# The second dense layer of a two-block transformer kernel: gates and ups in one phase and downs in another, each by seven products instead of eight

## The reference

```python
def swiglu(h, wg, wu, wd):
    return (jax.nn.silu(h @ wg) * (h @ wu)) @ wd
...
        h = rms_norm(x, norm_ffn_g[i]) * (1 + sc2) + sh2
        x = x + g2 * swiglu(h, ffn_w_gate[i], ffn_w_up[i], ffn_w_down[i])
    return rms_norm(x, final_norm_g)
```

## Time and profile before

| | us |
|---|---|
| median of 3 runs | 1472.97 (1471.86 to 1478.15) |
| the profiled execution | 1474.04 |
| its span | 1472.3 |
| TensorE matmul busy | 1382.5 (94%) |
| VectorE busy | 811.6 (55%) |
| ScalarE busy | 248.1 (17%) |
| mean granted clock of TensorE | 0.981 |

### The profile page before, as it was taken

One profiled execution on the slowest core, in us unless ns is written; L12 is line 12 of the kernel. 1 busy time (PEld: TensorE's weight loads), 2 busy tenths in 40 slices (PEclk: granted clock), 3 DMA queues, 4 the chain that ended last, 5 costly groups with the idle time before them and its releaser, 6 DMA issues. The chain is left out here.

```text
span 1472.3 us, 18919 instructions
## 1 busy us (share of the span) xinstructions
PE 1382.5 (94%) x7561; PEld 1018.4 (69%) x7561; DVE 811.6 (55%) x1405; ACT 248.1 (17%) x530; POOL 259.0 (18%) x342
## 2 busy tenths in 40 slices
PE   5999999988757999999999999999999999999997
PEld 1877655644333888778888888777776868777774
DVE  2458785332223677853544674888744963544432
ACT  2221211000001211322435101000002032000001
POOL 5078010000001100543436304000021000000000
PEclk9999999998888999999999999999999999999999
DMA  9976788899999588846773456988853633545530
GB/s 345 324 253 230 273 341 328 366 415 416 417 418 369 184 299 290 298 142 157 182 174 117 143 171 201 333 323 326 311 183 103 215 94 115 168 151 168 166 120 29
DMA packets 176055, 355.57 MB, mean 242 GB/s; under 512 B 7289, under 2 KB 137040, under 8 KB 158560
## 3 DMA queue, kind: packets, MB, share of 16 engines
q1 hardware_dynamic: 166720, 313.64, 59.8%
q0 software_dynamic: 9248, 40.71, 9.5%
HBM read 352.58 MB, written 1.74 MB: 241 GB/s over the span
## 5 line engine op out<-in xcount | busy, mean ns | idle before, releaser
L1823 PE MATMUL PS<-HT,ring 128*128 128x256 f32 x1152 | 258.3, 382 | 0.1
L1823 PEld LDWEIGHTS PS<-HT,ring 128*128 128x128 f32 x1152 | 215.5, 190 | 36.0 <-issue 7.9
L2724 PE MATMUL PS<-ring,hid 128*128 128x512 f32 x320 | 143.5, 592 | 0.0
L2724 PEld LDWEIGHTS PS<-ring,hid 128*128 128x128 f32 x320 | 60.8, 190 | 60.3 <-issue 58.4
L2718 PE MATMUL PS<-HT,ring 128*128 128x256 f32 x464 | 101.6, 379 | 0.0
L2718 PEld LDWEIGHTS PS<-HT,ring 128*128 128x128 f32 x464 | 87.8, 190 | 11.8
L1264 PE MATMUL PS<-ring_extra,slot_rows 128*32 128x256 f32 x576 | 54.6, 431 | 27.7 <-DMA ring_extra<-in_expert_w_gate 7.9
L1541 DVE TENSOR_TENSOR X<-X,PS 128x1024 f32<-128x1024 f32 x14 | 17.1, 1221 | 111.6 <-PE PS L1317 111.6
L2747 PE MATMUL PS<-ring,half_sums 128*128 128x256 f32 x288 | 68.1, 379 | 0.0
L2747 PE MATMUL PS<-ada_stage,half_sums 128*128 128x256 f32 x288 | 68.1, 379 | 0.0
L2747 PE MATMUL PS<-ring,HT 128*128 128x256 f32 x288 | 65.2, 379 | 0.0
(11 more groups left out here) (653 smaller groups left out, 2283.4 us busy)
## 6 DMA issues: line engine op xcount, KB each, us to landing
ring<-in_hy_w_in SPq DMA_DIRECT2D x40, 1024.0 KB, 7.5
ring_extra<-in_w_ada SPq DMA_DIRECT2D x24, 1024.0 KB, 8.5
ada_stage<-in_ada_w POOLq DMA_DIRECT2D x24, 1024.0 KB, 7.6
ring<-in_ffn_w_gate SPq DMA_DIRECT2D x22, 1024.0 KB, 5.7
ring<-in_ffn_w_up SPq DMA_DIRECT2D x22, 1024.0 KB, 5.9
ring<-in_ffn_w_down SPq DMA_DIRECT2D x22, 1024.0 KB, 5.1
ring_extra<-in_expert_w_down SPq DMA_DIRECT2D x18, 1024.0 KB, 22.9
ring_extra<-in_expert_w_up SPq DMA_DIRECT2D x18, 1024.0 KB, 20.1
```

Source lines behind the costliest of these rows:

```text
L1823: mm = pe.matmul(dst, w[:, k, half * P:(half + 1) * P], HT[:, k, :], start=(k == 0), stop=(k == KT - 1))
L2724: mm = pe.matmul(PS[:, 4 + 2 * i + h, :], hid[:, par, f, i * P:(i + 1) * P], w[:, f, h * 512:(h + 1) * 512], start=first and f == 0, stop= ...
```

## The change

In the second dense layer all 11 chunks take seven products for gate and up, and their products lie in banks 0 to 3 for even chunks and 4 to 7 for odd ones (`split_bank`). The downs are no longer mixed in. The turned rows of all chunks are kept (`hid_T`, in the memory of the finished accumulator `acc`), and so are four sums of halves of them (`hid_half`, 5, 4 and 2 chunks at a time). Then come all downs, with tokens, the 256 hidden and the 1024 columns in two halves each: seven products of one matmul of 128 x 512 per chunk, accumulated over the chunks in seven banks, in six groups of one or two chunks (`DOWN_GROUPS`). VectorE makes four sums of halves of each down weight, 512 wide, one of them in place. At the end `split_last` combines the seven banks into the four pieces of x. Chunk 10's rows are turned inside the first group of downs. The weights arrive in the order g0, u0, g1, u1, up to u10, then d0 to d10, and SP's loop is unrolled. The sums of chunk 0's weights are placed before the gating of the second pointwise product. A semaphore of an earlier stage becomes one that is given back after its stage.

```diff
-segment("ffn1", [ffn_source(1)(k, e) for k, e in expert_order(FFN_CHUNKS)])
+SPLIT_ORDER = [(k, e) for e in range(FFN_CHUNKS) for k in "gu"] + [("d", e) for e in range(FFN_CHUNKS)]
+segment("ffn1", [ffn_source(1)(k, e) for k, e in SPLIT_ORDER])
...
-sem("d_c"), pool_dma_sem("d_fetched"), sem("d_summed"), sem("d_cols"),
+sem("d_c"), sem("d_fetched"), sem("d_summed"), sem("d_cols"),
...
+down_ready = sem("d_ready")
+hid_T = carve(acc[:].rearrange("p a b -> p (a b)"), 0, [FFN_CHUNKS, 2, S])
+hid_half = carve(stage_conv, 0, [4, FFN_CHUNKS, P])
+down_sum = [(tap_blocks[:].rearrange("p a b c -> p (a b c)")[:, 0:12 * CW], wsum[:, 0].rearrange("p j k n -> p (j k n)"),
+             wsum[:, 1].rearrange("p j k n -> p (j k n)"))[b].rearrange("p (e j n) -> p e j n", e=2, j=3)
+            for b in range(3)]
+last_rows = tap_blocks[:].rearrange("p a b c -> p (a b c)").rearrange("p (a n) -> p a n", a=8)
...
 def chunk(f, kind, e):
-    return FFN_BASE[f] + order.index((kind, e))
+    return FFN_BASE[f] + (order, SPLIT_ORDER)[f].index((kind, e))
+
+ROWS_0 = 1 + 7 * NSEV
+HALF_SUMS = ROWS_0 + 2
+DOWN_GROUPS = ((0, 1), (2, 3), (4, 5), (6, 7), (8,), (9, 10))
+HALF_GROUPS = ((0, 5), (5, 9), (9, 11))
+DOWN_ORDER = ("P2", "P1", "P6", "P5", "P3", "P7", "P4")
+DOWN_BANK = {"P2": 4, "P1": 5, "P6": 6, "P5": 7, "P3": 0, "P7": 1, "P4": 2}
+
+def split_summed(e):
+    return ROWS_0 + 1 if e == 0 else split_row(e - 1, 1)
+
+def split_row(e, nth):
+    return HALF_SUMS + 1 + 7 * e + nth + 1
+
+def split_bank(e, name):
+    at = ("P1", "P2", "P5", "P3", "P6", "P4", "P7", "TURN").index(name)
+    return PS[:, 4 * (e % 2) + at // 2, at % 2 * CW:(at % 2 + 1) * CW]
...
-ffn(1, ffn_source(1))
+send_until(sp, FFN_BASE[1] + len(SPLIT_ORDER))
...
+def split_turn(e, m):
+    if m == 0:
+        pe.wait_ge(hid_ready, FFN_CHUNKS + e + 1)
+        pe.wait_ge(combined, split_row(e, 4))
+    else:
+        pe.wait_ge(silu_ready, ACT_MARKS[1, e + 1, ("move", 0)])
+    for i in range(TT):
+        mm = pe.transpose(split_bank(e, "TURN")[:, i * P:(i + 1) * P], hid_rows[:, e % 2, i, m * P:(m + 1) * P],
+                          ident[:])
+    mm.then_inc(sevens, 1)
+
+def split_gate_up(e, norm):
+    n_g, n_u = chunk(1, "g", e), chunk(1, "u", e)
+    gate, up = w_slot(n_g), w_slot(n_u)
+    half = lambda ap, h: [ap[:, 4 * h + k, :] for k in range(4)]
+    rows = lambda h, i: [HT[:, 4 * h + k, i * P:(i + 1) * P] for k in range(4)]
+    hs7 = lambda j: [hsum[:, j, k, :] for k in range(4)]
+    ws7 = lambda j: [wsum[:, (e + 1) % 2, j, k, :] for k in range(4)]
+    to = lambda name: split_bank(e, name)
+    arrive(pe, n_g)
+    arrive(pe, n_u)
+    pe.wait_ge(combined, split_summed(e))
+    if e == 0:
+        for name, h, done in (("P1", 0, left), ("P2", 1, right)):
+            for k in range(KT // 2):
+                pe.wait_ge(done, 4 * norm + k + 1)
+                mm = pe.matmul(to(name), rows(h, 0)[k], half(gate, h)[k], start=(k == 0), stop=(k == KT // 2 - 1))
+        mm.then_inc(used, 1)
+        pe.wait_ge(combined, HALF_SUMS)
+    else:
+        if e >= 2:
+            pe.wait_ge(combined, split_row(e - 2, 6))
+        product(to("P2"), rows(1, 0), half(gate, 1))
+        product(to("P1"), rows(0, 0), half(gate, 0)).then_inc(used, 1)
+    product(to("P5"), hs7(0), ws7(0))
+    if e:
+        split_turn(e - 1, 0)
+    else:
+        pe.wait_ge(combined, HALF_SUMS + 1)
+    product(to("P3"), hs7(3), half(up, 1))
+    if e:
+        split_turn(e - 1, 1)
+    product(to("P6"), hs7(1), ws7(1)).then_inc(sevens, 1)
+    if e >= 2:
+        pe.wait_ge(silu_ready, ACT_MARKS[1, e - 1, ("move", 1)])
+    product(to("P7"), hs7(2), half(up, 0)).then_inc(used, 1)
+    pe.wait_ge(combined, split_row(e, 2))
+    product(to("P4"), rows(1, 1), ws7(2)).then_inc(sevens, 1)
+
+def split_down(gi):
+    group = DOWN_GROUPS[gi]
+    for e in group:
+        arrive(pe, chunk(1, "d", e))
+    pe.wait_ge(down_ready, DOWN_MARKS["weights", gi])
+    pe.wait_ge(down_ready, DOWN_MARKS["rows", [e1 > group[-1] for _, e1 in HALF_GROUPS].index(True)])
+    if gi == 0:
+        pe.wait_ge(combined, split_row(LAST_E - 1, 6))
+        pe.wait_ge(silu_ready, ACT_MARKS[1, LAST_E, ("move", 1)])
+    for name in DOWN_ORDER:
+        if gi == 0 and name == "P3":
+            split_turn(LAST_E, 0)
+            pe.wait_ge(combined, split_row(LAST_E, 6))
+        if gi == 0 and name == "P7":
+            split_turn(LAST_E, 1)
+        for at, e in enumerate(group):
+            w, sums = w_slot(chunk(1, "d", e), D), down_sum[gi % 3][:, at]
+            a = lambda i, m: hid_T[:, e, m, i * P:(i + 1) * P]
+            b = lambda m, h: w[:, m, h * 512:(h + 1) * 512]
+            lhs, rhs = {"P1": (a(0, 0), b(0, 0)), "P2": (a(0, 1), b(1, 0)), "P3": (hid_half[:, 3, e], b(1, 1)),
+                        "P4": (a(1, 1), sums[:, 2]), "P5": (hid_half[:, 0, e], sums[:, 0]),
+                        "P6": (hid_half[:, 1, e], sums[:, 1]), "P7": (hid_half[:, 2, e], b(0, 1))}[name]
+            mm = pe.matmul(PS[:, DOWN_BANK[name], :], lhs, rhs, start=(e == 0), stop=(e == LAST_E))
+            if name == "P4":
+                mm.then_inc(used, 1)
+            elif e == LAST_E:
+                mm.then_inc(downed, 1)
...
-ffn(1, 2)
+for e in range(FFN_CHUNKS):
+    split_gate_up(e, 2)
+for gi in range(len(DOWN_GROUPS)):
+    split_down(gi)
...
-ffn(1)
+for e in range(FFN_CHUNKS + 1):
+    if e <= LAST_E:
+        act.wait_ge(combined, split_row(e, 0))
+        act.activation(gate_act[:, e % 2, 0], gate_pre[:, 0], ACT.Silu).then_inc(silu_ready, 1)
+    if e:
+        for m in range(2):
+            act.wait_ge(sevens, PE_MARKS[1, e, ("turn", m)])
+            act.activation(hid_T[:, e - 1, m, :], split_bank(e - 1, "TURN"), ACT.Copy).then_inc(silu_ready, 1)
+    if e <= LAST_E:
+        act.wait_ge(combined, split_row(e, 6))
+        act.activation(gate_act[:, e % 2, 1], gate_pre[:, 1], ACT.Silu).then_inc(silu_ready, 1)
+act.wait_ge(downed, 3 + 2)
+act.activation(last_rows[:, 0, :], PS[:, DOWN_BANK["P1"], :], ACT.Copy).then_inc(silu_ready, 1)
...
+def split_sum_weights(e):
+    for n in (chunk(1, "g", e), chunk(1, "u", e)):
+        dve.wait_ge(landed[slots[n]], 16 * turns[n])
+    if e >= 2:
+        dve.wait_ge(sevens, PE_MARKS[1, e - 2, "P4"])
+    gate, up = w_slot(chunk(1, "g", e)), w_slot(chunk(1, "u", e))
+    t1, t2, t4 = (wsum[:, (e + 1) % 2, j] for j in range(3))
+    step(dve.tensor_tensor(t1, up[:, 0:4, :], gate[:, 0:4, :], ALU.subtract))
+    step(dve.tensor_tensor(t2, up[:, 4:8, :], t1, ALU.subtract))
+    step(dve.tensor_tensor(up[:, 0:4, :], up[:, 4:8, :], up[:, 0:4, :], ALU.subtract))
+    dve.tensor_tensor(t4, gate[:, 4:8, :], t2, ALU.subtract).then_inc(combined, 1)
+
+def split_sum_down(gi):
+    for at, e in enumerate(DOWN_GROUPS[gi]):
+        n = chunk(1, "d", e)
+        dve.wait_ge(landed[slots[n]], 16 * turns[n])
+        if gi >= 3:
+            dve.wait_ge(used, chunk(1, "d", DOWN_GROUPS[gi - 3][-1]) + 1)
+        w = w_slot(n, D)
+        t1, t2, t4 = (down_sum[gi % 3][:, at, j] for j in range(3))
+        b11, b12, b21, b22 = (w[:, m, h * 512:(h + 1) * 512] for m in range(2) for h in range(2))
+        step(dve.tensor_tensor(t1, b12, b11, ALU.subtract))
+        step(dve.tensor_tensor(t2, b22, t1, ALU.subtract))
+        step(dve.tensor_tensor(b12, b22, b12, ALU.subtract))
+        last = dve.tensor_tensor(t4, b21, t2, ALU.subtract)
+        if e == DOWN_GROUPS[gi][-1]:
+            last.then_inc(down_ready, 1)
+
+def split_halve_rows(at):
+    e0, e1 = HALF_GROUPS[at]
+    dve.wait_ge(silu_ready, ACT_MARKS[1, e1, ("move", 1)])
+    a11, a12, a21, a22 = (hid_T[:, e0:e1, m, i * P:(i + 1) * P] for i in range(TT) for m in range(2))
+    out = lambda j: hid_half[:, j, e0:e1, :]
+    step(dve.tensor_tensor(out(0), a21, a22, ALU.add))
+    step(dve.tensor_tensor(out(2), a11, a21, ALU.subtract))
+    step(dve.tensor_tensor(out(1), out(0), a11, ALU.subtract))
+    dve.tensor_tensor(out(3), a12, out(1), ALU.subtract).then_inc(down_ready, 1)
+
+def split_combine(e):
+    of = lambda name: split_bank(e, name)
+    dve.wait_ge(used, chunk(1, "g", e) + 1)
+    step(dve.tensor_copy(gate_pre[:, 0], of("P2")))
+    dve.tensor_tensor(gate_pre[:, 0], of("P1"), gate_pre[:, 0], ALU.add).then_inc(combined, 1)
+    if e < LAST_E:
+        split_sum_weights(e + 1)
+    else:
+        dve.wait_ge(combined, split_row(e, 0))
+        dve.sem_inc(combined, 1)
+        split_sum_down(0)
+    dve.wait_ge(sevens, PE_MARKS[1, e, "P6"])
+    step(dve.tensor_copy(up_pre[:, 0], of("P1")))
+    dve.tensor_tensor(up_pre[:, 0], of("P6"), up_pre[:, 0], ALU.add).then_inc(combined, 1)
+    dve.wait_ge(combined, split_row(e, 2))
+    step(dve.tensor_tensor(up_pre[:, 1], of("P5"), up_pre[:, 0], ALU.add))
+    dve.tensor_tensor(up_pre[:, 1], of("P3"), up_pre[:, 1], ALU.add).then_inc(combined, 1)
+    dve.wait_ge(combined, split_row(e, 3))
+    dve.wait_ge(silu_ready, ACT_MARKS[1, e, ("gate", 0)])
```

(83 more changed lines are left out.)

## The result

The changed kernel takes 1468.34 us (median of 8, 1466.74 to 1469.60), the kernel before 1475.74 in the runs beside it (8, 1471.86 to 1478.15): a ratio of 0.9946, 95% interval 0.9933 to 0.9960. The forecast was 1466.0 from a median of 1472.97, a ratio of 0.9953.

A forecast was written before the change was run, and what follows sets the result against it. TensorE was taken to bound the stage, VectorE having over half its time free. Products -12.01, waits +2.66 and end +2.33 gave -7.02 us, so 1466.0 us (-0.47%), range 1462.8 to 1470.6.

The forecast's parts named there:

- The products: TensorE's work in the second dense layer: fewer gate, up and down matmuls, two more chunks' rows turned; together -12.01 us.
- Steady chunks: First-phase chunks other than 0, 8 and 10: period 12.53 us, no wait, 0.25 us to spare before P4.
- Three waits: TensorE waits before P4 for VectorE's up row sum in chunks 0, 8 and 10: +1.16, +0.96, +0.54, sum +2.66 us.
- the 0.32: Delay from the end of VectorE's row sum to P4's start: 0.10 handoff plus 0.22 us weight load.
- The variant in that step: If TensorE resumes without the 0.22 us load, waits before P4 in chunks 0, 8 and 10 sum to 2.0 us.
- rival 1: Small waits before P4 are less, 2.66 falling to about 0.5 us; time 1463.8 us; chance 0.12.
- The downs: Second phase, six groups of down products: VectorE never the later one, loads with some 9 us of cover, no wait.
- rival 4: Loads of the downs land late, chunk 10's sums 7.8 us late; time 1473.8 us; chance 0.02.
- The end: Last add to x starts 3.25 us after T, TensorE's last issue, by nine VectorE steps from P3; before 0.92; +2.33.
- Rival 2: The 0.25 us margin before P4 is missing, so every steady chunk waits; +3.5 us, time 1469.5; chance 0.20.
- Rival 3: Short waits lower TensorE's clock to 0.91 in the first phase or the downs too; 1479.6 or 1486.2 us; chance 0.03.
- the side given 0.38: Overall result faster by over 0.5%, below the edge at 1465.6 us, chance 0.38; within 0.5% had 0.59.

The follow-up runs named there:

- the downs by eight: Changed kernel with eight down matmuls a chunk into banks 4 to 7, no sums for downs, old end; layer time 215.23 us, ratio to before 0.9974.
- the fifth sum: Changed kernel plus one 1024-wide VectorE sum, written to unused memory, ahead of the up row sum in chunks 0 to 9; layer time 222.08 us against 209.23.
- The chunk order of the last group: Changed kernel with chunk 8's P7 and P4 down matmuls done in the last group, with those of 9 and 10; layer time 207.96 us against 209.23.
- the repeat: The changed kernel, unaltered, measured again on another occasion; 1470.34 us (median of 7), ratio to before 0.9954, layer time 209.22 us.

## Why the prediction was right

- **The products** were forecast at -12.01 us. The layer's other terms measure 2.12 (waits) and 2.20 (end), and -7.68 - 2.12 - 2.20 = -12.00. The downs' part was checked alone (the downs by eight), and the two chunks with their turns are what that kernel has left.
- **Steady chunks** have the forecast period (12.53; 12.52) and no wait. The room in them was forecast at 0.25 us. By the fifth sum it is 1.26 + 0.10 - 0.86 = 0.50. The same term was mis-sized here: with 0.06 in place of 0.32 the forecast's own sum gives 0.51.
- **Three waits** were forecast in the right chunks, for the right sum, at 1.16, 0.96 and 0.54; they are 0.88, 0.76 and 0.48. The term that was mis-sized is the 0.32 between the end of VectorE's sum and P4's start. P4 starts 0.06 after the sum and loses 0.10 within its matmuls, 0.16 in all: loading the weights after the wait doesn't cost the 0.22 by which they are loaded ahead. That is 0.16 in each of the three; the small rest is that the sum itself ends 0.12 and 0.05 earlier than forecast in chunks 0 and 8, and 0.08 later in chunk 10. The variant in that step, without the 0.22 of the load, gave 2.0 and was nearer; it is a quarter of the way to rival 1. The ops themselves were as computed: 0.82 for the width of 640, interpolated 0.83. The Trainium skill (VectorE: DVE Perf Modes, section on the errata of SBUF sources) has a formula for f32 sums; the estimate from it was 0.82, and the trace agrees.
- **The downs** ran without a wait and without a late load: 66.57 us busy of 66.57. So rival 4 isn't there.
- **The end** was forecast at T + 3.25 and is T + 3.12, nine steps in a row from P3 on, from 1453.40. The nine took 6.28 instead of 6.48 and began 0.07 later. It cost 2.20 of 2.33. The chunk order of the last group shows that it was those steps: with P3 1.72 us earlier the end moved 1.27.
- **Rival 2**, a late row sum in every chunk, isn't there, and it was priced too high: with a room of 0.50 a row sum 0.5 later would cost a steady chunk 0.1 at most, not 0.25. Its direction was right: the fifth sum, 1.26 later, costs 0.86 in each of eight chunks, and even without the 3.38 that the clock took the layer's whole gain would be gone.
- **Rival 3**, the clock: 1.00 throughout the layer. Cycling through eight banks or through four is the same to 0.01 us, and waits of 0.59 us in each of eight chunks left the clock at 1.00. The Trainium skill (TensorE: Matmul & The Clock Gate, section on psum-queue depth-cycling) tells of a kernel in bf16 whose clock oscillated as it cycled through banks and idled a little between groups; this trace, in f32, shows nothing of the kind. Longer pauses did lower it: 1.87 us twice, 5.94 once, and 1.91 before the transposes in one execution of eleven.
- **Where the total came out**: the layer gained 7.68 us, 0.52% of 1475.74, and the measured 0.54% lies 0.07 points beyond the forecast of 0.47%. Both are on the edge of 0.5% on which the chances were split. The first measurement falls on the side given 0.38 and the repeat, 0.46%, on the one given 0.59, so on which side it came out is luck; the mechanism and its terms are not.

What was not tried: seven products for chunks 0 and 10 alone with the old mixing of downs, and P4 in a bank of its own. And why the work ahead of the layer varies by 5.6 us between executions of like code stays open, but for the 1.25 us that the clock took in one of them.
